# Hybrid decoder block: six tiles of the third norm go through DRAM and VectorE's block transpose instead of TensorE

## The reference, cut to what matters

```python
gu = h @ w_gate_up[i]
x = x + (jax.nn.silu(gu[..., :D_FF]) * gu[..., D_FF:]) @ w_down[i]
gate = jax.nn.sigmoid(rmsnorm(x, g_ple_gate[i]) @ w_ple_gate[i])
e = rmsnorm(p[i].astype(x.dtype) @ w_ple_up[i], g_ple_post[i])
x = x + gate * e
...
return rmsnorm(x, g_final)
```

## Time and profile before

| | |
|---|---|
| median of 3 runs | 999.38 us (999.04 to 999.69) |
| the profiled execution: its time, its span | 1000.92 us, 999.0 us |
| TensorE busy | 987.9 us, 99% of the span |
| VectorE, ScalarE, GpSimd busy | 705.0, 459.4, 384.7 us |
| granted TensorE clock, mean | 0.997 of full speed |
| chain of waits that ended last | 92% TensorE, 3% VectorE, 1% each ScalarE, GpSimd, DMA |

### The profile page before, as it was taken

One profiled execution on the slowest core, in us unless ns is written; L12 is line 12 of the kernel. 1 busy time (PEld: TensorE's weight loads), 2 busy tenths in 40 slices (PEclk: granted clock), 3 DMA queues, 4 the chain that ended last, 5 costly groups with the idle time before them and its releaser, 6 DMA issues.

```text
span 999.0 us, 12373 instructions
## 1 busy us (share of the span) xinstructions
PE 987.9 (99%) x4511; PEld 819.0 (82%) x4511; DVE 705.0 (71%) x969; ACT 459.4 (46%) x706; POOL 384.7 (39%) x288
## 2 busy tenths in 40 slices
PE   9999999999999999999999999999999999999996
PEld 7888888888887888888888888888888888888885
DVE  6899999967799355354454444543687888985887
ACT  7625447413363333423333333333445665575775
POOL 3446797711146544444444354351000000011745
PEclk9999999999999999999999999999999999999998
DMA  7421202685525134233333332413998787632222
GB/s 256 141 82 43 82 4 105 212 211 163 153 64 159 53 112 124 81 106 112 99 106 98 114 106 82 130 64 118 366 382 292 239 310 257 195 107 105 85 85 107
DMA packets 120735, 142.46 MB, mean 143 GB/s; under 512 B 22826, under 2 KB 77634, under 8 KB 120674
## 3 DMA queue, kind: packets, MB, share of 16 engines
q1 hardware_dynamic: 120528, 141.40, 43.2%
q10 hardware_dynamic: 146, 0.27, 0.1%
HBM read 106.77 MB, written 34.87 MB: 142 GB/s over the span
## 4 chain that ended last, share of the span: by engine, by line
PE 92%; DVE 3%; issue 2%; ACT 1%; DMA 1%; POOL 1%; SPq 0%; POOLq 0%; ACTq 0%; DVEq 0%
PE ps L1604 30%; PE ps L1606 30%; PE ps L1605 30%; PE ps L1658 1%; DMA raw<-in_w_in 1%; DVE ftmp L2465 0%; ACT junk L1017 0%; DVE resid L2468 0%; DVE spare L2006 0%; PE ps L1762 0%; PE ps L1752 0%; DVE raw_b L2236 0%; DVE raw_b L2230 0%; POOL rs L747 0%; PE ps L1742 0%
## 5 line engine op out<-in xcount | busy, mean ns | idle before, releaser
L744 POOL TENSOR_SCALAR ss<-ss 128x1 f32<-128x1 f32 x38 | 17.7, 467 | 317.1 <-ACT junk L1017 295.8
L2100 DVE SCALAR_TENSOR_TENSOR ps<-resid,convw,ps 128x512 f32<-128x512 f32 x190 | 127.2, 748 | 0.0
L1604 PE MATMUL ps<-ring_hi,ring_lo 128*128 128x512 f32 x308 | 120.0, 390 | 0.1
L1606 PE MATMUL ps<-ring_hi 128*128 128x512 f32 x308 | 119.8, 389 | 0.0
L1605 PE MATMUL ps<-ring_lo,ring_hi 128*128 128x512 f32 x308 | 119.8, 389 | 0.0
L1604 PE MATMUL ps<-act_hi,bs_lo 128*128 128x512 f32 x240 | 93.6, 390 | 0.0
L1606 PE MATMUL ps<-act_hi,bs_hi 128*128 128x512 f32 x240 | 93.4, 389 | 0.0
L1605 PE MATMUL ps<-act_lo,bs_hi 128*128 128x512 f32 x240 | 93.4, 389 | 0.0
L2251 DVE TENSOR_TENSOR gtmp<-ps,gtmp 128x512 f32<-128x512 f32 x22 | 15.2, 691 | 95.5 <-PE ps L1606 95.5
L1003 ACT ACTIVATE ring_hi<-raw 128x512 fp32r<-128x512 f32 x89 | 51.9, 625 | 58.9 <-PE ps L1606 58.8
L750 POOL TENSOR_TENSOR wc_lo<-raw_b,wc_hi 128x1024 fp32r<-128x1024 f32 x22 | 56.1, 2552 | 49.9 <-ACT wc_hi L1003 48.7
(11 more groups left out here) (281 smaller groups left out, 2640.7 us busy)
## 6 DMA issues: line engine op xcount, KB each, us to landing
raw<-in_w_gate_up SPq DMA_DIRECT2D x44, 512.0 KB, 5.2
raw<-in_scratch SPq DMA_DIRECT2D x52, 256.0 KB, 3.3
raw<-in_w_down SPq DMA_DIRECT2D x52, 256.0 KB, 4.0
in_scratch<-in_s SPq DMA_DIRECT2D x44, 256.0 KB, 3.3
in_scratch<-gtmp SPq DMA_DIRECT2D x33, 256.0 KB, 2.4
keep<-in_w_down SPq DMA_DIRECT2D x32, 256.0 KB, 4.0
keep<-in_scratch SPq DMA_DIRECT2D x25, 256.0 KB, 3.5
resid<-in_x SPq DMA_DIRECT2D x8, 512.0 KB, 7.1
```

The source lines that it names most:

```text
L744: pool.tensor_scalar(ss[:, n:n + 1], ss[:, n:n + 1], 1.0 / D, EPS, ALU.mult, ALU.add)\
L1604: pe.matmul(dst, w_lo_, m_hi, start=start, stop=False, skip_group_check=onto)
L1606: return pe.matmul(dst, w_hi_, m_hi, start=False, stop=stop, skip_group_check=onto)
L2100: dve.scalar_tensor_tensor(out=conv_c if k == last_odd else acc, in0=u_all[:, c, k + h * BANK:k + (h + 1) * BANK], scalar=convw[:, c * 32 ...
```

## The change

Tiles 0, 1, 2, 3, 4 and 6 of the third norm are no longer turned by TensorE. SyncE stores each to a new DRAM tensor (`store_xg`), loads it back in eight DMAs of 64 KB with the 32x32 blocks transposed (`load_xg`), and VectorE turns the blocks into the same PSUM banks with two transposes of 128x512 (`gate_turn`). Tiles 5 and 7 stay with TensorE. Four of the eight loads of tile 1 are issued by ScalarE. `even_high(0)` moves behind the last two `step_hi`, `gate_norm(2)`, `(3)`, `(4)` and `(6)` move up, two of the last four `step_sum` move down, and `gate_22(m)` stands ahead of `sums(m + 1)` instead of behind it.

```diff
+    xg_dram = nc.dram_tensor("xg_scratch", (TT, 2, P, BANK), F32, kind="Internal").ap()
...
+        DVE_TURNS = (0, 1, 2, 3, 4, 6)
+        def load_xg(queue, t, parts=range(P // SQ)):
+            queue.wait_ge(xn_stored[t % 2], DMA * (HT_MIX // 2 + t // 2 + 1))
+            for a in parts:
+                for h in range(2):
+                    src = xg_dram[t, h].rearrange("(b j) (k a i) -> a j k b i", j=SQ, a=P // SQ, i=SQ)[a]
+                    queue.dma_start(xg_place(t)[a * SQ:(a + 1) * SQ, h, :].rearrange("j (k b i) -> j k b i", k=4, i=SQ),
+                                    src).then_inc(xn_in[t % 2], DMA)
+            def store_xg(t):
+                sp.wait_ge(xn_ok, 2 * TT + t + 1)
+                sp.dma_start(xg_dram[t].rearrange("h p n -> p h n"), xg_place(t)).then_inc(xn_stored[t % 2], DMA)
...
+            store_xg(0)
+            load_xg(sp, 0)
+            store_xg(1)
+            load_xg(sp, 1, range(0, 2))
+            store_xg(2)
             sp.wait_ge(ed_mm, 4 * STEPS)
             load_e(0)
-            sp.dma_start(raw_b[:, 0, :], g_ple_post[0].partition_broadcast(P)).then_inc(gain_in, DMA)
+            sp.dma_start(raw_b[:, 0, :], g_ple_post[0].partition_broadcast(P)).then_inc(rawb_in, DMA)
+            load_xg(sp, 2, range(0, 2))
+            store_xg(3)
+            load_xg(sp, 2, range(2, 4))
             load_e(1)
+            load_xg(sp, 3)
             sp.dma_start(raw_b[:, 1, :], g_final.partition_broadcast(P)).then_inc(gain_in, DMA)
             load_e(2)
+            store_xg(4)
+            load_xg(sp, 4)
             next_e(3)
             next_e(4)
             store_out(0)
             store_out(1)
+            store_xg(6)
+            load_xg(sp, 6)
             next_e(5)
...
-                if n == 6 * PAIRS + 8:
-                    even_high(0)
...
+            even_high(0)
+            gate_norm(2)
+            load_xg(act, 1, range(2, 4))
             a21_copy(0)
             odd_high(0)
+            gate_norm(3)
             sum_high(0, 6)
             gate_p1(0)
...
             square_odd(4)
-            gate_norm(2)
-            gate_norm(3)
             gate_u2(0)
             sigmoid(0, c11_ok, QUADS + 1)
             even_high(1)
+            gate_norm(4)
             gate_p5(0)
...
-                if pi == 6 and j == 6:
-                    turn(0, 2)
...
-            turn(1, 2)
...
                 gate_part(m, 6)
-                if m + 1 < PAIRS_G:
-                    turn(2 * m + 2, 2)
                 gate_part(m, 5)
-                if m + 1 < PAIRS_G:
+                if m in (1, 2):
                     turn(2 * m + 3, 2)
...
+            def gate_turn(t):
+                dve.wait_ge(xn_in[t % 2], DMA * (P // SQ) * (HT_MIX // 2 + 2 * (t // 2 + 1)))
+                if t in (0, 1, 3):
+                    dve.wait_ge(ed_ok, {0: 24, 1: 26, 3: 28}[t])
+                else:
+                    dve.wait_ge(fs4_ok, FS + t // 2)
+                    dve.wait_ge(fa_lo, FA + 3 * (t // 2) - 1)
+                bank = 2 if t % 2 == 0 else odd_bank(t // 2)
+                for j in range(2):
+                    dve.transpose(ps[:, bank + j, :], xg_place(t)[:, j, :]).then_inc(xn_turned, 1)
...
                 if n == 6 * PAIRS + 9:
-                    even_low(0)
-            for m in range(4):
-                step_sum(6, m)
+                    gate_turn(0)
+            even_low(0)
+            step_sum(6, 0)
+            step_sum(6, 1)
+            gate_turn(1)
```

More of the change, by code:

```diff
@@ L158, in turns, with dve_turns @@
         def turns(n):
-            return 2 * (n if n < TT + HT_MIX else max(n - HT_MIX, TT))
+            by_dve = sum(TT <= k < TT + HT_MIX or 0 <= k - 2 * TT and k - 2 * TT in DVE_TURNS for k in range(n))
+            return 2 * (n - by_dve)
+        DVE_TURNS = (0, 1, 2, 3, 4, 6)
+        def dve_turns(t):
+            return HT_MIX + 2 * DVE_TURNS.index(t)
         def block_turned(t):
@@ L951, in times_post @@
                 if t == 0:
-                    pool.wait_ge(gain_in, 4 * DMA)
+                    pool.wait_ge(rawb_in, 4 * DMA)
                 e = e_place(t)
@@ L1359, in gate_norm @@
                 act.wait_ge(rs_ok, n + 1)
-                if t >= 2:
+                if t == 7:
                     act.wait_ge(turned, turns(n - 1))
+                elif t >= 2:
+                    act.wait_ge(xn_turned, dve_turns(t - 2) + 2)
                 else:
@@ L1366, in even_high @@
             def even_high(m):
-                n = 2 * TT + 2 * m
                 for j in range(2):
-                    act.wait_ge(turned, turns(n) + j + 1)
+                    act.wait_ge(xn_turned, dve_turns(2 * m) + j + 1)
                     if m:
@@ L1376, in a21_copy @@
             def a21_copy(m):
-                act.wait_ge(turned, turns(2 * TT + 2 * m + 1) + 1)
+                if m < 2:
+                    act.wait_ge(xn_turned, dve_turns(2 * m + 1) + 1)
+                else:
+                    act.wait_ge(turned, turns(2 * TT + 2 * m + 1) + 1)
                 act.wait_ge(fs1_ok, FS + m)
@@ L1382, in odd_high @@
             def odd_high(m):
-                act.wait_ge(turned, turns(2 * TT + 2 * m + 1) + 2)
+                if m < 2:
+                    act.wait_ge(xn_turned, dve_turns(2 * m + 1) + 2)
+                else:
+                    act.wait_ge(turned, turns(2 * TT + 2 * m + 1) + 2)
                 if m:
@@ L1544, in _ @@
                     square_odd(7)
-                gate_norm(2 * m + 2)
                 square_out(2 * m - 2)
@@ L1551, in _ @@
                 even_high(m + 1)
+                if m == 1:
+                    gate_norm(6)
                 gate_p5(m)
@@ L1571, in _ @@
             act.wait_ge(fs4_ok, FS + m + 1)
-            act.wait_ge(gain_in, 4 * DMA)
+            act.wait_ge(gain_in, 3 * DMA)
             copy(pair(2), raw_b[:, 1, :], gain_ok)
@@ L2421, in sums @@
                 dve.tensor_tensor(x_sum(7), quarter(2), g_a21, ALU.subtract).then_inc(fs3_ok, 1)
-                dve.wait_ge(turned, turns(2 * TT + 2 * m + 1) + 2)
+                if m < 2:
+                    dve.wait_ge(xn_turned, dve_turns(2 * m + 1) + 2)
+                else:
+                    dve.wait_ge(turned, turns(2 * TT + 2 * m + 1) + 2)
                 if m == 0:
@@ L2472, in final @@
                 if t == 0:
-                    dve.wait_ge(gain_in, 4 * DMA)
+                    dve.wait_ge(gain_in, 3 * DMA)
                 x_ = x_tile(t, 3)[:, c]
@@ L2481, in _ @@
             sum_low(0, 5)
+            step_sum(6, 2)
+            step_sum(6, 3)
             gate_11(0)
@@ L2485, in _ @@
             odd_low(0)
+            gate_turn(2)
             even_low(1)
+            gate_22(0)
+            gate_turn(3)
             sums(1)
-            gate_22(0)
             last_sum(1)
@@ L2499, in _ @@
                 odd_low(m)
+                gate_turn(2 * m + 2)
                 final(2 * m - 2)
@@ L2502, in _ @@
                 even_low(m + 1)
+                gate_22(m)
                 sums(m + 1)
-                gate_22(m)
                 last_sum(m + 1)
```

11 lines of the change are left out of this document (2 added, 9 removed).

## The result

| | before | after |
|---|---|---|
| median, both on one chip, 13 runs each | 999.46 us (998.99 to 1000.23) | 1001.3 us (999.19 to 1002.97) |
| ratio, 95% interval | | 1.0016 (1.0009 to 1.0023) |
| profiled execution: time, span | 1000.92, 999.0 us | 1002.64, 1000.6 us |
| mean granted clock | 0.997 | 0.994 |

The changed kernel is slower by 0.16%, within the 0.2% named ahead as no change but on the other side of it, and 5.7 us above the forecast, outside the range (994.0 to 999.4). Its executions spread over 3.8 us, those of before over 1.2, and they go with their mean granted clock: 999.19 and 999.39 us at 0.998, 1002.52 to 1002.97 at 0.994. The profiled one is among the slowest, 1.3 us above the median.

The account below looks back on a forecast made before the run. TensorE, busy 99% of the span, was taken to bound the kernel. Turns saved 5.3 us, less waits of 0.5, 0.2 and 0.8, gave 3.8 us less: 999.38 to 995.6 us, range 994.0 to 999.4.

Parts of the forecast that it names:

- six turns: TensorE's transposes of six tiles in the third norm: removing them was to save 5.3 us.
- tile 1 late, part 6 of pair 0: First pair: tile 1's data lands at 908.0, so TensorE waits 0.5 us for the lo half of sum 6.
- part 5 of pair 0: First pair: gate_11(0) now stands behind sums and steps on VectorE, so TensorE waits 0.2 us.
- part 3 of pair 0: First pair: gate_p5(0) level with TensorE, put at 0, 0.3 us at worst; a wait would show the forecast wrong.
- part 5 of the last pair: Last pair: TensorE comes one turn earlier and waits 0.8 us for gate_11(3) on VectorE.
- the later pairs: Pairs after the first: tile data in time, only VectorE's time remains, costing 0.8 us at gate_11(3).
- Tiles 3, 4 and 6 have 5 us and more between landing and use: Pairs after the first: these tiles' loads from DRAM arrive at least 5 us before VectorE needs them.
- the slower rival: DRAM round trip of 6.2 us a store, then 9.6: 7.8 us of waits, 2.5 us slower, 1001.9 us; chance 0.11.
- the rival of double price: VectorE's transposes into PSUM cost 2.5 us a tile: 3.9 us back, 999.5 us, no change; chance 0.07.
- A turn's price: TensorE's eight transposes of one tile: 0.885 us, taken from the profile instead of the skill's 2.2 us.
- By itself it is worth nothing: Moving gate_22(m) ahead of the sums gains nothing alone, but covers 2.2 us of delay at part 4.

Follow-up runs that it names:

- the control: The changed kernel timed again unaltered, on another chip: 1001.84 us, ratio 1.0015 to the kernel before.
- the halves: Changed kernel with gated(0) done in two halves and gate_p1(1) waiting for the first only: 1000.73 us, ratio 1.0003 to the kernel before.
- tile 3 back: Changed kernel with tile 3 turned by TensorE again: 997.6 us, ratio 0.9977 to the kernel before; repeated on another chip 998.56 us, 0.9988.
- tiles 0, 1, 4, 6: Changed kernel with only these four tiles turned by VectorE, tiles 2 and 3 by TensorE again: 997.52 us, ratio 0.9977 to the kernel before.
- the fill: Changed kernel with 12 unused small matmuls put ahead of part 6 of pair 1: 1000.12 us, ratio 1.0001 to the kernel before.
- tile 6 back: Changed kernel with tile 6 turned by TensorE again: 1003.77 us, ratio 1.0032 to the kernel before.
- tiles 0 and 1: Changed kernel with only these two tiles turned by VectorE, 2, 3, 4 and 6 by TensorE again: 998.64 us, ratio 0.9991 to the kernel before.
- gate_22 back too: Changed kernel with only tiles 0 and 1 turned by VectorE and gate_22 behind the sums again: 998.79 us, ratio 0.9987 to the kernel before.

## Why the prediction was wrong

The sum against the stage, in us:

| term | forecast | measured |
|---|---|---|
| six turns | -5.3 | -5.3 (48 records less) |
| tile 1 late, part 6 of pair 0 | 0.5 | 0 |
| part 5 of pair 0 | 0.2 | 0 |
| part 3 of pair 0 | 0 | 0.18 (0.97 in the control) |
| part 6 of pair 1 | none | **3.35** |
| clock behind it | none | **2.83** (1.5 in the control) |
| part 5 of the last pair | 0.8 | 1.10 |
| sum | -3.8 | +2.16 (stage +2.23) |

**The step that failed** is the part on the later pairs, "What remains is VectorE's time", which then looks at `gate_11` and `gate_22` alone. It asks whether tiles 3, 4 and 6 land in time and reads the margins of `gate_11(2)`, `gate_11(3)` and `gate_22`. It never goes to the start of each part of pair 1 and asks what it waits for. Part 6 waits for `gate_p1(1)`, that for `gated(0)`, and the margin was 0 before. The term missing from the sum is nearly the whole gain of the four turns ahead of it, 3.35 us. Shown by: the halves (1.2 us taken from that dependence alone shorten the wait by 1.0), tile 3 back, and tiles 0, 1, 4, 6 (no wait).

**Two readings of the same part** failed with it. "Tiles 3, 4 and 6 have 5 us and more between landing and use" was wrong for tile 3: VectorE asked for it at 920.71 and had it at 922.62. And tile 2, said to land before VectorE asks at 917.5, was asked for at 915.29 and there at 916.48. The forecast of 916 for its landing was about right; VectorE was 2 us ahead of the forecast, as tile 1 was on time. Tile 2's lateness goes on to `even_high(1)` and `gate_p5(0)`, and so to the wait of part 3 that the forecast had called a sign of being wrong: tile 2's transposes start 29.21 us after `gate_norm(0)` in after, with 0.18 us of wait, and 29.99 in the control, with 0.97.

**The clock** stood in the forecast only as an addition to the slower rival. That it hangs on the idle time is shown by the fill. It is not one price: 2.83 us in one trace of after and 1.5 in the other, behind the same wait. That it is missing in the fastest executions of after (999.19 us at 0.998) is likely by their clocks, and no trace shows it.

**The slower rival** named another mechanism, a slow round trip through DRAM. It did not occur. SyncE of after, against the earlier trace rows: 2.8 us from the store to the first load, where 3.3 was taken, and 0.66 us an issue where 0.55 was.

```profile
888.44 0.38 SPq L718 DMA_DIRECT2D xg_scratch<-keep  x1
891.23 5.32 SPq L530 DMA_DIRECT2D keep<-xg_scratch  x8
896.60 0.63 SPq L718 DMA_DIRECT2D xg_scratch<-keep  x1
899.69 3.19 SPq L530 DMA_DIRECT2D keep<-xg_scratch  x4
```

Tile 0 was there at 898.38 (forecast 899.9; this execution runs 0.7 us ahead of that of before). **Tile 1** was there when VectorE came to it, at 905.84 (forecast 908.0), for a reason that the forecast had not: it counted ScalarE's four issues behind `gate_norm(2)`, but they ran beside it. ScalarE and its queue:

```profile
899.31 1.06 ACT L1036 ACTIVATE spare<-ps 128x512 fp32r<-128x512 f32 x2
899.83 0.68 ACTq L530 DMA_DIRECT2D keep<-xg_scratch  x1
900.26 1.15 ACT L1036 ACTIVATE keep<-resid,rs 128x1024 f32<-128x1024 f32 x1
900.54 2.07 ACTq L530 DMA_DIRECT2D keep<-xg_scratch  x3
```

VectorE of after, against the earlier trace rows: two transposes of 128x512 into PSUM take 1.32 us, as taken (1.3), so the rival of double price falls. Tile 1's need no wait for its data:

```profile
898.38 1.32 DVE L2426 STREAM_TRANSPOSE ps<-keep 128x512 f32<-128x512 f32 x2 [0.89 <-DMA keep<-xg_scratch]
...
905.84 1.32 DVE L2426 STREAM_TRANSPOSE ps<-keep 128x512 f32<-128x512 f32 x2
```

**A turn's price** of 0.885 us was right: four less with 1.14 of waits give -2.46, two less -1.79 (0.89 each). The Trainium skill ("TensorE: Matmul & The Clock Gate", Part 4: PE-mode transpose) gives about 275 ns for one transpose in a kernel. Taken as a price for each of eight, an estimate from it is 2.2 us a turn and 4.4 for two; the 1.79 measured for two shows that the price does not add up so here.

**The last pair** was mis-sized: 1.10 for 0.8. With tile 6 back on TensorE it is still 0.65, and with `gate_22` at its old place as well (tiles 0 and 1) it is gone; the move makes VectorE wait 1.22 us for TensorE's part 7 in that pair, which reaches `gate_11(3)`. "By itself it is worth nothing" was wrong there: without the transposes it costs 0.65. VectorE with tiles 0 and 1, then with gate_22 back too:

```profile
963.75 0.69 DVE L2504 TENSOR_TENSOR ftmp<-ps,ftmp 128x512 f32<-128x512 f32 x1 [1.22 <-PE ps L1642]
```

```profile
965.17 0.68 DVE L2504 TENSOR_TENSOR ftmp<-ps,ftmp 128x512 f32<-128x512 f32 x1
```

**What stays open.** Why the waits of the versions with tile 3 back add up to 2.3 to 2.5 us in three different orders: VectorE, ScalarE and GpSimd pass on each other's delays, and no run takes one of them out. And why the clock is low in most executions of tile 6 back, and differs from one execution of after to the next; one execution of each run has a trace.
